# Values stationary in a block attention, a later turn in a latent attention, and a weight piece fetched earlier

## What is computed

```
# block attention; with 256 tokens every query sees its own block, causally
s_own = einsum('bhqd,bhnd->bhqn', q_c, k_own) * scale + table[:, rel_bucket(d_own)]
p     = softmax(where(d_own >= 0, s_own, NEG_INF))
y_a   = einsum('bhqn,bhne->bhqe', p, v_own)
merged = sigmoid(z_a) * (y_a @ w_br_attn) + sigmoid(z_r) * (y_r @ w_br_ret) + sigmoid(z_m) * (y_m @ w_br_mem)

# memory attention: its keys and values come from rmsnorm(mem)
k, v = split(rmsnorm(mem, g_mem) @ w_mem_kv, 2)

# latent attention: two low-rank projections, then per head
cq, ckv, kpe, z = split(rms_norm(x) @ w_in, ...)
kv = rms_norm(ckv) @ w_ukv
s  = einsum('bqhd,bkhd->bhqk', q, k) * scale          # blockwise causal mask
o  = einsum('bhqk,bkhd->bqhd', softmax(s), v) * silu(z)
x + o @ w_out
```

## Time and profile before

| | |
|---|---|
| median of 3 runs | 795.5 us (795.1 to 795.79) |
| the profiled execution: its own time | 795.22 us |
| its span, first to last instruction | 793.4 us |
| mean granted TensorE clock | 1.000 |
| PE busy | 777.7 us |
| DVE, ACT, POOL busy | 562.7, 434.6, 132.3 us |

### The profile page before, as it was taken

The page is one execution under the profiler, slowest core; times in us unless marked ns, Lnnn a source line. Parts: engine busy times, 40 slices in busy tenths (PEclk is TensorE's granted clock), DMA queues, the critical chain, the costliest instruction groups (busy, mean ns, idle before and its releaser), DMA issues.

```text
span 793.4 us, 11940 instructions
## 1 busy us (share of the span) xinstructions
PE 777.7 (98%) x4616; PEld 686.7 (87%) x4616; DVE 562.7 (71%) x911; ACT 434.6 (55%) x594; POOL 132.3 (17%) x103
## 2 busy tenths in 40 slices
PE   9999999999999999999999999999999999999998
PEld 7788888888888899999988888999799878978886
DVE  5655666885468687787874385689965896887785
ACT  6754544345443575556644374555756335889650
POOL 0002920000000005444441000023005000016000
PEclk9999999999999999999999999999999999999999
DMA  9986434334454565555545536435474415644311
GB/s 340 408 289 248 166 134 159 127 141 158 164 198 169 192 238 199 187 186 174 199 161 210 183 136 212 159 117 189 164 261 161 159 59 207 232 143 157 107 54 54
DMA packets 23364, 142.78 MB, mean 180 GB/s; under 512 B 3564, under 2 KB 4472, under 8 KB 7312
## 3 DMA queue, kind: packets, MB, share of 16 engines
q1 hardware_dynamic: 20160, 134.51, 47.5%
q10 hardware_dynamic: 1776, 4.12, 1.4%
q0 software_dynamic: 1376, 3.43, 1.2%
HBM read 140.97 MB, written 2.64 MB: 181 GB/s over the span
## 4 chain that ended last, share of the span: by engine, by line
PE 82%; DVE 10%; ACT 3%; DMA 2%; issue 2%; SPq 0%; ACTq 0%; DVEq 0%
PE gemm L493 17%; PE gemm L495 16%; PE gemm L494 16%; PE gemm L499 8%; PE gemm L501 8%; PE gemm L500 8%; DVE wlo L1682 3%; DMA raw<-in_weights 2%; ACT whi L1171 2%; DVE xc L2210 1%; PE head L757 1%; PE head L559 1%; PE head L682 1%; PE head L733 1%; DVE xmlo L1837 1%
## 5 line engine op out<-in xcount | busy, mean ns | idle before, releaser
L1682 DVE TENSOR_TENSOR wlo<-raw,whi 128x2048 fp32r<-128x2048 f32 x121 | 280.4, 2318 | 106.0 <-ACT whi L1171 105.8
L1171 ACT CAST whi<-raw 128x2048 fp32r<-128x2048 f32 x121 | 230.7, 1907 | 192.6 <-PE gemm L495 112.9
L493 PE MATMUL gemm<-whi,x0hi 128*128 128x512 f32 (+2 forms) x400 | 157.1, 393 | 1.4 <-DVE wlo L1682 1.4
L495 PE MATMUL gemm<-whi,x0lo 128*128 128x512 f32 (+2 forms) x400 | 153.9, 385 | 0.0
L494 PE MATMUL gemm<-wlo,x0hi 128*128 128x512 f32 (+2 forms) x400 | 153.6, 384 | 0.0
L499 PE MATMUL gemm<-x1hi,whi 128*128 128x256 f32 x400 | 113.6, 284 | 0.0
L501 PE MATMUL gemm<-x1hi,wlo 128*128 128x256 f32 x400 | 113.2, 283 | 0.0
L500 PE MATMUL gemm<-x1lo,whi 128*128 128x256 f32 x400 | 113.2, 283 | 0.0
L493 PEld LDWEIGHTS gemm<-whi,x0hi 128*128 128x128 f32 x400 | 75.1, 188 | 17.6 <-DVE wlo L1682 2.3
L495 PEld LDWEIGHTS gemm<-whi,x0lo 128*128 128x128 f32 x400 | 75.0, 188 | 14.8
L494 PEld LDWEIGHTS gemm<-wlo,x0hi 128*128 128x128 f32 x400 | 75.3, 188 | 13.4
(11 more groups left out here) (362 smaller groups left out, 1330.7 us busy)
## 6 DMA issues: line engine op xcount, KB each, us to landing
raw<-in_weights SPq DMA_DIRECT2D x122, 1024.0 KB, 4.7
raw<-in_weights SPq DMA_DIRECT2D x4, 512.0 KB, 6.1
bias_rows<-bias_row POOLq DMA_DIRECT2D x1, 1536.0 KB, 19.8
memt<-in_memt SPq DMA_DIRECT2D x4, 256.0 KB, 5.1
tok<-in_mem SPq DMA_DIRECT2D x1, 1024.0 KB, 7.0
xt<-in_xt SPq DMA_DIRECT2D x2, 512.0 KB, 11.4
xres<-in_x ACTq DMA_DIRECT2D x1, 1024.0 KB, 8.9
bias<-bias_rows POOLq DMA_DIRECT2D x8, 128.0 KB, 5.0
```

The source lines that it names most:

```text
L493: mm(o, xh, wh, start=start, stop=False)
L495: return mm(o, xl, wh, start=False, stop=stop)
L1171: nc.scalar.copy(whi[:, p % RING, :], raw[:, p % RING, :]).then_inc(s_hi, 1)
L1682: V.tensor_tensor(wlo[:, p % RING, :], raw[:, p % RING, :], whi[:, p % RING, :].bitcast(F32), ALU.subtract).then_inc(s_lo, 1)
```

## The change

It has three parts, and none of them changes what is computed.

1. Block attention. The probabilities are divided by their sum before they are turned (`head_divide`, DVE, after the weight split of the step), and the turn waits for that (`moba_probs_divided`). Two heads are weighed together (`weigh_pair`), with the values as the stationary operand: one head's result goes to partitions 0 to 63 and the other's to 64 to 127 of the same bank, already turned. ACT and DVE split it from there into `x1hi`, `x1lo`. The turns "ya" and their splits are gone.
2. Latent attention. For heads 4 to 7 `mla_turn` stands in the middle of the half piece (`mid`), not ahead of it. In step `p0("cu") + 3` the weight split is done in two halves, with `turn_lo("ckv")` between them (`PARTED`).
3. Start. `next_piece(3)` stands ahead of the transfers of the memory's tokens and of the parameters, and the memory's norm moves from step 0 to step 1.

The diff, cut (left out: renamed semaphores, and the places where "ya" is only dropped from a tuple):

```
-SCALED = {"mem": 0, "mix": 3, "ckv": p0("cu") + 3, "cq": p0("ukv")}
+SCALED = {"mem": 1, "mix": 3, "ckv": p0("cu") + 3, "cq": p0("ukv")}
+PARTED = p0("cu") + 3
...
             sp.wait_ge(s_half_piece[1], 16)
+            next_piece(3)
             sp.dma_start(tok[:, 12:14, :, :].rearrange("p a b c -> p (a b c)"), ins["mem"]).then_inc(s_mem, 16)
             sp.dma_start(par[:, GAINS:NPAR], ins["params"][:, GAINS:NPAR]).then_inc(s_par, 16)
-            next_piece(3)
...
-                pe.wait_ge(s_jx, n + 1)
+                if JOBS[j][0] == "moba":
+                    pe.wait_ge(s_jr, j + 1)
+                else:
+                    pe.wait_ge(s_jx, n + 1)
...
+            def weigh_pair(h):
+
+                j = job("moba", h)
+                if h > 1:
+                    pe.wait_ge(s_yalo, h // 2)
+                pe.wait_ge(s_jpe, j + 1)
+                if h == 1:
+                    chunk_free(pe, c0("qkv") + 2)
+                for k, keys, queries in ((0, slice(0, S), slice(0, S)), (1, slice(S, TRI), slice(P, S))):
+                    for n in (0, 1):
+                        i = mm(A[3][n * 64:n * 64 + 64, queries], tok[:, 2, k, (h - 1 + n) * 64:(h + n) * 64],
+                               prob_t[:, n, keys], start=k == 0, stop=k == 1)
+                i.then_inc(s_yo, 1)
...
+                if kind == "moba":
+                    if h % 2:
+                        weigh_pair(h)
+                    return
...
                 for j in range(4):
+                    if j == 2 and mid:
+                        mid()
...
                 for h in range(2):
+                    if h and mid:
+                        mid()
...
-                    if e < MLA_H:
+                    if e < 4:
                         mla_turn(e)
                     for k in ((0, 1), (2,), (3,))[e] if e < 3 else ():
                         mla_pe_turn(k)
+                    mid = (lambda: mla_turn(e)) if 4 <= e < MLA_H else None
...
+                if head_at(p - 3) and head_at(p - 3)[0] == "moba" and head_at(p - 3)[1] % 2:
+                    h = head_at(p - 3)[1]
+                    act.wait_ge(s_yo, h // 2 + 1)
+                    act.wait_ge(s_mm, p0("qkv"))
+                    nc.scalar.copy(x1hi[:, h // 2, :], A[3][:, 0:S]).then_inc(s_yahi, 1)
...
+            def split_part(p, h):
+
+                dve.wait_ge(s_hi, p + 1)
+                c = slice(h * D, h * D + D)
+                return V.tensor_tensor(wlo[:, p % RING, c], raw[:, p % RING, c],
+                                       whi[:, p % RING, c].bitcast(F32), ALU.subtract)
...
+                if head_at(p - 3) and head_at(p - 3)[0] == "moba" and head_at(p - 3)[1] % 2:
+                    h = head_at(p - 3)[1]
+                    dve.wait_ge(s_yahi, h // 2 + 1)
+                    V.tensor_tensor(x1lo[:, h // 2, :], A[3][:, 0:S], x1hi[:, h // 2, :].bitcast(F32),
+                                    ALU.subtract).then_inc(s_yalo, 1)
+
+            def head_divide(p):
+
+                if head_at(p - 1) is None or head_at(p - 1)[0] != "moba":
+                    return
+                j = job(*head_at(p - 1))
+                dve.wait_ge(s_jx, j + 1)
+                order(V.reciprocal(rsum[:, :], psumr[:, j % 4, :]))
+                for t, (a, b) in enumerate(((0, P), (P, TRI))):
+                    i = V.tensor_scalar(prob[:, j % 2, a:b], prob[:, j % 2, a:b], rsum[:, t:t + 1], None, ALU.mult)
+                i.then_inc(s_jr, 1)
...
-                if p not in LATE_SPLIT and p > 0:
+                if p == PARTED:
+                    split_part(p + 2, 0)
+                    boundary(p)
+                    split_part(p + 2, 1).then_inc(s_lo, 1)
+                elif p not in LATE_SPLIT and p > 0:
                     split(p + 2)
+                head_divide(p)
```

More of the change, by code:

```diff
@@ L302, in program @@
             "probs_turned", "probs_turned_copied", "head_weighed", "head_done"))
+        s_yo, s_yahi, s_yalo, s_jr = (sem(n) for n in (
+            "moba_pair_weighed", "moba_y_hi", "moba_y_lo", "moba_probs_divided"))
         s_rot, s_ident, s_half = sem("rotated"), sem("ident_loaded"), sem("halves_ready")
@@ L365, in fills @@
             return base, (kb + 1) // 2, kb
-        DEST = {"ya": (x1hi, x1lo, 0),
-                "yr": (x1hi, x1lo, 4), "ym": (x0hi, x0lo, 4), "merged": (x0hi, x0lo, 0),
+        DEST = {"yr": (x1hi, x1lo, 4), "ym": (x0hi, x0lo, 4), "merged": (x0hi, x0lo, 0),
                 "ffn": (x1hi, x1lo, 0), "ml": (x0hi, x0lo, 0), "mla": (x0hi, x0lo, 0),
@@ L382, in turn_bank @@
         def turn_bank(name, i):
-            return A[0] if name in ("ya", "yr", "ym") else A[i]
+            return A[0] if name in ("yr", "ym") else A[i]
         def turn_source(name, t, kb):
@@ L392, in turn_source @@
                 return cu[:, t, a:a + P]
-            if name in ("ya", "yr", "ym"):
-                return tok[:, {"ya": 0, "yr": 3, "ym": 7}[name], t, c]
+            if name in ("yr", "ym"):
+                return tok[:, {"yr": 3, "ym": 7}[name], t, c]
             return tok[:, 10 + kb // 4, t, (kb % 4) * P:(kb % 4) * P + P]
@@ L399, in turn_steps @@
             found = [("cq", range(2))] if p == CQ_STEP else []
-            for n, s in (("ya", 26), ("yr", 28), ("ym", 32)):
+            for n, s in (("yr", 28), ("ym", 32)):
                 if p in (s, s + 1):
@@ L535, in turn @@
                             pe.wait_ge(s_hg, 2 * (i // 2) + t + 1)
-                    if name == "ya":
-                        pe.wait_ge(s_jn, job("moba", MOBA_H - 1) + 1)
+                    if name == "yr":
                         pe.wait_ge(s_jte, len(TURNED))
-                    if name == "yr":
-                        pe.wait_ge(s_jn, job("ret", RET_H - 1) + 1)
+                        pe.wait_ge(s_jn, RET_H)
                     if name == "ym":
-                        pe.wait_ge(s_jn, job("mem", MEM_H - 1) + 1)
+                        pe.wait_ge(s_jn, RET_H + MEM_H)
                     if name == "merged":
@@ L740, in head_weigh @@
                 kind, h = head_at(p - 3)
+                if kind == "moba":
+                    if h % 2:
+                        weigh_pair(h)
+                    return
                 j = job(kind, h)
-                if j >= 1:
-                    pe.wait_ge(s_jn, j)
+                if j == MOBA_H:
+                    pe.wait_ge(s_yalo, 4)
+                else:
+                    pe.wait_ge(s_jn, j - MOBA_H)
                 if kind == "ret":
@@ L925, in mla_o_turn, with z_unit @@
                 last.then_inc(s_ot, 1)
-            def z_unit(e):
+            def z_unit(e, mid=None):
                 p, t = piece_of(e), e % 2
@@ L943, in z_unit, with out_unit @@
                     i.then_inc(s_mm, 1)
-            def out_unit(e):
+            def out_unit(e, mid=None):
                 p, t = piece_of(e), e % 2
@@ L981, in mla_tail @@
                         mla_pe_turn(k)
+                    mid = (lambda: mla_turn(e)) if 4 <= e < MLA_H else None
                     if e < 6:
-                        z_unit(e)
+                        z_unit(e, mid)
                     else:
-                        out_unit(e)
+                        out_unit(e, mid)
             def keep_awake():
@@ L1072, in _ @@
                     if i_ % 2 == 0:
-                        pe.wait_ge(s_tlo, sum(fills(("ya", "yr", "ym")[i_ // 2])[:2]))
+                        if i_ == 0:
+                            pe.wait_ge(s_yalo, 4)
+                        else:
+                            pe.wait_ge(s_tlo, sum(fills(("yr", "ym")[i_ // 2 - 1])[:2]))
                     chunk_free(pe, c - 2)
@@ L1926, in head_dve @@
             def head_dve(p):
-                if head_at(p - 3):
+                if head_at(p - 3) and head_at(p - 3)[0] != "moba":
                     kind, h = head_at(p - 3)
                     j = job(kind, h)
-                    dve.wait_ge(s_jo, j + 1)
+                    dve.wait_ge(s_jo, j - MOBA_H + 1)
                     if kind == "ret":
@@ L2299, in _ @@
                     angles()
-                boundary(p)
+                if p != PARTED:
+                    boundary(p)
                 for name, step in SCALED.items():
```

14 lines of the change are left out of this document (6 added, 8 removed).

## The result

The changed kernel takes 797.27 us (median of 22 runs, 795.45 to 798.67) beside 795.52 us for the kernel before (median of 22, 795.1 to 796.36). The ratio is 1.0019, 95% interval 1.0013 to 1.0025: slower by 0.2%, where I had said 793.7. Its profiled execution took 796.48 us with a span of 794.7 (before 795.22 and 793.4).

What follows compares the result with a forecast made beforehand. PE bounds the kernel, busy 777.7 of 793.4 us. Terms +2.4 - 2.0 + 0.9 - 1.1 - 1.9 = -1.7 us against 795.22 give 793.5, 793.7 as a median; range 791.2 to 796.2.

Steps and rivals of the forecast that it cites:

- The start: Ahead of piece 4: its split comes late behind the memory's squares and norm, piece 4 begins at 33.8, +2.4 us.
- the clock falls in the new gap: Rival, ahead of piece 4: PE's 3.8 us standstill brings back the slow beginning that cost 1.8 us; 795.5, 11%.
- Block attention, PE: PE instructions of weighing and turns: 4.9 and 0.9 us removed, four pairs at 0.95 added, -2.0 us.
- the 0.1 for going in: Block attention: allowance of 0.1 us per weighed pair for going into it, on top of the scores' 0.85.
- the 0.2 in the bound: Block attention: 0.2 us for changing the array's division, within the upper bound of 1.5 us for a pair.
- that rival: Block attention: column halves don't overlap, a pair costs 1.5 us, 2.2 more in all; 795.9, no change, 11%.
- The division: Block attention: the turn of the probabilities waits for DVE's division behind the weight split, +0.9 us, from 0 to 2.
- my slower rival: Turns of all eight heads: each division waits behind a POOL instruction, each turn 0.6 late, 4.8 us; 797.6, 8%.
- Before the latent attention: First latent projection: with half the split ahead of it, `cqlo` starts sooner and -1.1 of its 1.3 us wait goes.
- the tail: Latent attention's turns: half a unit of matmuls ahead removes three waits for `olo` and their restarts, -1.9 us.
- The clock's case: Forecast if the gap ahead of piece 4 brings the slow beginning back at full length: 795.5, no change, 11%.

Runs made afterwards that it cites:

- the filled gap: Changed kernel with 32 instructions of unused matmuls on ones between the small matmul behind piece 3 and piece 4: 795.49 us.
- the old start: Changed kernel with only the move of the fourth piece undone: 793.10 us; the kernel with only the new block attention has this start too.
- the squares early: Changed kernel with the memory's squares (ScalarE) and norm (VectorE) ahead of the split of the columns of x in step 1: 792.89 us.
- the start alone: Kernel before with only the move of the fourth piece, `next_piece(3)`, and of the memory's norm: 801.07 us.
- the block attention alone: Kernel before with only the block attention part of the change: 796.33 us.
- divisions first: Changed kernel with the memory's squares and norm early, and on VectorE `head_divide(p)` ahead of the weight split `split(p + 2)`: 790.79 us.

## Why the prediction was wrong

**The start: right to 0.4 us.** Piece 4 at 33.8 was predicted, with a gap of 3.8; it was 34.20 with 3.96. 0.3 of the 0.4 is the landing of the columns of x, 23.06 for 22.78. It varies between executions with this start: 22.35, 22.99, 23.26 and 25.17 in four other profiles.

**The step that failed: "the clock falls in the new gap", a rival with 11% at +1.8 us.** It was the case. The sum priced 3.8 us of standing still at 3.8 us less its cover, and nothing behind it; I held against the fall only that no wait in the kernel before, none over 1.4 us, had brought it, which says nothing of a gap nearly three times as long. It costs 1.5 us in the profiled execution and 1.8 in the median against the filled gap. The chance was wrong. The size was right, in part by luck: it was taken from one row of 5.33 us for the first 32 matmuls, which take 5.29 to 6.72 us in this study's 13 profiles (1.7 to 3.1 us more than at 0.112 each), and at which the profile lists a granted clock of 1.00, so that they are slow for the same reason isn't shown. The Trainium skill (TensorE: Matmul & The Clock Gate, What's actually happening) says that idle time puts the array back to 1.2 GHz; the granted clock of 0.50 behind 3.96 us agrees.

**Block attention, PE: -2.0 predicted, -2.0 by the rows.** The pair is 0.80 us, and 0.94 with 0.09 more in front of its first matmul and 0.05 more behind the turn that follows it: the predicted 0.95, of which neither the 0.1 for going in nor the 0.2 in the bound had a row. The column halves do overlap, so that rival is out: at the steps of 0.11 and 0.22 us the eight instructions would be 1.3 us in a row. They don't overlap in full either. By the tiles' independence alone (the Trainium skill, TensorEngine Tiling (Array Packing), Key Properties) a pair would be 0.65; with the sentence there on draining the engine at a change of mode the 0.09 and 0.05 us at its two ends agree. What the 0.15 between 0.65 and 0.80 is, no run here shows.

**The division, the second step that failed: +0.9 predicted, 1.9 by the starts in the changed kernel, 2.4 to 2.5 with the old start.** The sum was too small by its own terms: 0.4 us and three times 0.2 to 0.5 are 1.0 to 1.9, and I wrote 0.9. The mechanism is right, split behind `x1lo`, division behind the split. I foresaw steps 13, 15, 17 and 19. Step 13, which waits for the division of step 12, was given 0.4 and costs 0.7, step 15 costs 0.9, and 17 and 19 cost 0.14 each. Ahead of the first two the pair of multiplications takes 0.83 and 1.32 us. Behind 107 us, when GpSimd's rotary has ended, each takes 0.55, and the division is done only just too late. So my slower rival had a part of the mechanism, for two heads of eight. There is also a wait that I had at nothing, at the head of step 12: by the profile's label 1.0 us with the old start, 1.37 with the squares early, none in the changed kernel. It hangs on the bias by DMA, and I had not read what VectorE waited for in step 11.

**Before the latent attention and the tail: right.** -1.1 and -1.9 were predicted, -3.05 measured together.

**The sum.** For the profiled execution 793.5 was predicted and 796.48 measured, 3.0 us more: 1.5 for the clock, 1.0 for the division, 0.4 for the start, which leaves 0.1. The median lies 0.8 us above that execution, where I had allowed 0.3, since twelve of the 22 runs have the clock of 0.996. The parts measured one by one (+5.4, +0.7, -3.05) add to +3.0 where together they give +1.75. Of the 1.3 us between, about 0.6 is that the late start covers the wait for the bias, and part is that four of the five runs of the start alone have the lower clock; the rest is open. The clock's case had been worked out at 795.5, with every other term at its forecast. With the other two terms as they came out it would have been 796.9, above the range, which ended at 796.2.

## What to carry to other kernels

Before a change that opens a gap in front of TensorE, compare the gap with the longest one that the mean clock of 1.000 vouches for. If it is longer, add the matmuls behind it at the 1.2 GHz rate (here 1.5 us and more), or shorten it: filling half of this one already kept the clock up in nine runs of eleven.

A transfer that is asked for earlier displaces others, and the work in order behind them displaces more. Look at the queue of the engine that waits longest (here 3.7 us for the columns, 3.45 us for x) and put what is ready ahead of that wait. Two such moves and one of a short operation ahead of a long one made 789.4 us of 797.3.

Where a new operation links an engine to the critical path, read what that engine waits for now, even where it costs nothing now. And count a wait by the distance between starts: the profile's label left 0.7 us of 1.9 out here.

## What was not expected of the hardware

- The fall behind a gap isn't of one size. The same program had a mean clock of 0.998 in ten runs and 0.996 in twelve, and the times go with it (medians 796.5 and 798.0 us). With half of the gap filled it was 0.998 in two runs of eleven and 0.999 to 1.000 in nine. And once it was 0.998 without such a gap, in one run of eleven of the block attention alone.
- Useless matmuls that filled about half of the gap, or nearly all of it, cost nothing, since TensorE waits there anyway, and gave 1.5 and 1.8 us back in the median.
- VectorE's two multiplications on the probabilities, 128 and 256 columns, took 0.55 us without GpSimd's work beside them and up to 1.58 with its rotary beside them (divisions first), 2.9 times; the split of 2048 columns took up to 2.82 for 2.29. GpSimd's times go the same way: in the changed kernel three rotary instructions that run beside a split take 2.67 to 2.78 us, the other 21 take 0.72 to 0.86. No experiment took the rotary away, so that it is the cause is read from the times alone.
